# Key norms' roots taken two blocks at a time, and a pair's four loads issued at four points of the recurrence

## What is computed

```
r = (xr @ w_r)
k = (xk @ w_k)
v = (xv @ w_v)
kk = kf * k_k
kk = kk / jnp.maximum(jnp.sqrt(jnp.sum(jnp.square(kk), axis=-1, keepdims=True)), 1e-12)
k_dir = kf[None] * (1.0 + (a_rate - 1.0) * k_a)
y_f = wkv7_scan(r, decay[0], k_dir[0], v, -kk, kk * a_rate[0], reverse=False)
y_b = wkv7_scan(r, decay[1], k_dir[1], v, -kk, kk * a_rate[1], reverse=True)
# wkv7_scan, for each head of 64 channels:
#   sa = S @ a_t;  S = S * w_t + sa b_t^T + v_t k_t^T;  y_t = S @ r_t
```

## Time and profile before

| | us |
|---|---|
| median of 3 runs | 1931.05 (1930.81 to 1932.45) |
| the profiled execution, its own time | 1928.18 |
| its span in the trace | 1926.4 |
| PE busy | 1859.2 (97%) |
| DVE busy | 1055.7 (55%) |
| ACT busy | 755.4 (39%) |
| projections of k and v | about 895 to 1000 |
| recurrence | about 1000 to 1370 |

### The profile page before, as it was taken

The page is one execution under the profiler, slowest core; times in us unless marked ns, Lnnn a source line. Parts: engine busy times, 40 slices in busy tenths (PEclk is TensorE's granted clock), DMA queues, the critical chain, the costliest instruction groups (busy, mean ns, idle before and its releaser), DMA issues.

```text
span 1926.4 us, 38666 instructions
## 1 busy us (share of the span) xinstructions
PE 1859.2 (97%) x17053; PEld 1529.8 (79%) x17053; DVE 1055.7 (55%) x1405; ACT 755.4 (39%) x1006; POOL 174.2 (9%) x136
## 2 busy tenths in 40 slices
PE   6999899999999999999999999999999999999997
PEld 4898558778888888775679898899787788888886
DVE  5897665444432443447648888787664344324422
ACT  4434674334421332323844343343643353213322
POOL 1000002000000000210003211111120010000000
PEclk9999999999999999999999999999999999999999
DMA  6227223112332232443441111112352132332221
GB/s 213 84 72 233 77 99 131 66 44 91 106 110 87 88 110 90 153 137 126 153 140 50 50 50 51 50 47 69 125 197 88 33 99 87 110 103 88 94 88 44
DMA packets 165503, 189.41 MB, mean 98 GB/s; under 512 B 11801, under 2 KB 152646, under 8 KB 163674
## 3 DMA queue, kind: packets, MB, share of 16 engines
q1 hardware_dynamic: 162016, 174.44, 28.2%
q0 software_dynamic: 3088, 12.45, 1.6%
q10 hardware_dynamic: 234, 0.06, 0.0%
HBM read 161.22 MB, written 21.51 MB: 95 GB/s over the span
## 4 chain that ended last, share of the span: by engine, by line
PE 48%; DVE 5%; issue 2%; ACT 2%; DMA 0%; ACTq 0%; DVEq 0%; SPq 0%
PE ps L357 10%; PE ps L359 10%; PE ps L358 10%; PE ps L2353 7%; PE ps L2319 2%; PE ps L2366 2%; PE ps L2307 1%; PE ps L1743 1%; PE ps L2330 1%; PE ps L1313 1%; PE ps L2412 1%; PE ps L2449 1%; PE ps L1294 1%; DVE s_inverse_t L2683 1%; PE ps L2286 1%
## 5 line engine op out<-in xcount | busy, mean ns | idle before, releaser
L344 DVE TENSOR_TENSOR weights_split<-w,weights_split 128x2048 fp32r<-128x2048 f32 x116 | 265.7, 2290 | 235.3 <-ACT weights_split L326 230.5
L326 ACT ACTIVATE weights_split<-w 128x2048 fp32r<-128x2048 f32 x118 | 225.5, 1911 | 288.7 <-PE ps L359 270.2
L357 PE MATMUL ps<-x_hn_hi,weights_split 128*128 128x512 f32 x640 | 252.7, 395 | 0.0
L359 PE MATMUL ps<-x_hn_hi,weights_split 128*128 128x512 f32 x640 | 249.2, 389 | 0.0
L358 PE MATMUL ps<-x_hn_lo,weights_split 128*128 128x512 f32 x640 | 249.0, 389 | 0.0
L357 PE MATMUL ps<-f_hidden_hi,weights_split 128*128 128x512 f32 x512 | 199.3, 389 | 0.0
L359 PE MATMUL ps<-f_hidden_hi,weights_split 128*128 128x512 f32 x512 | 199.2, 389 | 0.0
L358 PE MATMUL ps<-f_hidden_lo,weights_split 128*128 128x512 f32 x512 | 199.2, 389 | 0.0
L1563 DVE SCALAR_TENSOR_TENSOR f_relu<-ps,x_squares 128x512 f32<-128x512 f32 x64 | 44.1, 691 | 191.1 <-PE ps L359 172.5
L358 PEld LDWEIGHTS ps<-x_hn_lo,weights_split 128*128 128x128 f32 x640 | 120.2, 188 | 26.2 <-issue 1.4
L357 PEld LDWEIGHTS ps<-x_hn_hi,weights_split 128*128 128x128 f32 x640 | 120.2, 188 | 26.0 <-issue 1.4
(11 more groups left out here) (365 smaller groups left out, 3513.6 us busy)
## 6 DMA issues: line engine op xcount, KB each, us to landing
w<-in_ffn_w_up_dram SPq DMA_DIRECT2D x32, 1024.0 KB, 5.4
w<-in_ffn_w_down_dram SPq DMA_DIRECT2D x32, 1024.0 KB, 4.8
w<-in_xattn_w_kv_dram SPq DMA_DIRECT2D x15, 1024.0 KB, 5.5
w<-in_ab_w_in_dram SPq DMA_DIRECT2D x10, 1024.0 KB, 5.0
w<-in_xattn_w_q_dram SPq DMA_DIRECT2D x8, 1024.0 KB, 4.9
w<-in_xattn_w_o_dram SPq DMA_DIRECT2D x8, 1024.0 KB, 4.7
w<-in_ab_w_out_dram SPq DMA_DIRECT2D x4, 1024.0 KB, 5.3
w<-in_rwkv_w_r_dram SPq DMA_DIRECT2D x4, 1024.0 KB, 6.5
```

What stands on the lines that cost most here:

```text
L326: act.activation(hi, raw, ACT.Copy).then_inc(k.w_hi_ready, 1)
L344: eng.tensor_tensor(lo, raw, hi.bitcast(F32), ALU.subtract).then_inc(k.w_lo_ready, 1)
L357: pe.matmul(out, lhs[0], rhs[0], start=start, stop=False)
L359: return pe.matmul(out, lhs[1], rhs[0], start=False, stop=stop)
```

## The change

There are two edits.

1. In the projections ACT no longer takes a root in every step t from 2 to 9. In the odd steps 3, 5, 7 and 9 it takes two, of blocks t - 3 and t - 2: Ln, Ln, one wait for both, Exp, Exp. DVE's multiplication of a key block by its root moves from step b + 3 to b + 4.
2. In the recurrence the four loads of a pair q no longer stand together at `bn` of pair q - 2. v stays there; kk is issued at `ua` of pair q - 2, r at `ub` of pair q - 2, and k at `qb` of pair q - 1, each after a wait for that copy. For q = 0 and 1 nothing changes.

```
-                if 2 <= t < 10:
+                if 3 <= t < 11 and t % 2:
 
-                    b = t - 2
-                    k.wait_freed(act, num[("n", b)])
-                    k.act.link(act, act.activation(rn[:, b % 4, :], rn[:, b % 4, :], ACT.Ln))
-                    act.activation(rn[:, b % 4, :], rn[:, b % 4, :], ACT.Exp, scale=-0.5).then_inc(s_rt, 1)
+                    b = t - 3
+                    for n in (b, b + 1):
+                        k.wait_freed(act, num[("n", n)])
+                        k.act(act.activation(rn[:, n % 4, :], rn[:, n % 4, :], ACT.Ln))
+                    k.act.wait(act)
+                    for n in (b, b + 1):
+                        act.activation(rn[:, n % 4, :], rn[:, n % 4, :], ACT.Exp, scale=-0.5).then_inc(s_rt, 1)
...
-                if 3 <= t < 11:
-                    b = t - 3
+                if 4 <= t < 12:
+                    b = t - 4
                     dve.wait_ge(s_rt, b + 1)
                     dve.tensor_tensor(kk[:, b, :], kk[:, b, :], rn[:, b % 4, :], ALU.mult).then_inc(s_kk, 1)
...
-def load_pair(k, sp, p):
+def load_pair(k, sp, p, rows=range(4)):
 
-    for a, src in enumerate((k.d_r, k.d_kk, k.d_k, k.d_v)):
+    for a in rows:
+        src = (k.d_r, k.d_kk, k.d_k, k.d_v)[a]
         sp.dma_start(k.pin[:, p % 2, a, :], src[:, p, :]).then_inc(k.s_pin[p % 2], 16)
...
                     if p + 2 < C:
                         full(sp, "VT", p)
-                        load_pair(k, sp, p + 2)
+                        load_pair(k, sp, p + 2, [3])
+                elif kind in ("ua", "ub", "qb"):
+
+                    q = p + 1 if kind == "qb" else p + 2
+                    if 2 <= q < C:
+                        taken(sp, kind.upper(), p)
+                        load_pair(k, sp, q, [{"ua": 1, "ub": 0, "qb": 2}[kind]])
```

## The result

The changed kernel takes 1949.72 us (median of 5 runs, 1944.13 to 1952.55) beside 1932.45 us for the kernel before (1930.81 to 1936.07). The ratio is 1.0083, with a 95% interval of 1.0059 to 1.0106: 0.6 to 1.1% slower, some 16 us by the ratio (the medians lie 17.3 apart). The forecast was 1939 with a range of 1930 to 1952. The span of the profiled execution went from 1926.4 to 1943.3 us, by 16.9.

The account below looks back on a forecast made before the run. PE, busy for 97% of the span, was taken to bound the kernel. The terms -5.0 + 13.7 + 3 - 2 - 2 = +7.7 us on 1931.05 gave about 1939 us, with a range of 1930 to 1952.

Parts of the forecast that it names:

- the likeliest case: Whole kernel: the forecast's own case, all five terms summing to +7.7 us, 1935 to 1946 us; chance 0.55.
- Edit 1, -5.0: Projections, at v0: fewer table loads on ACT save 3.3 us of waiting and 1.7 us of half clock, -5.0 us.
- The walk's five starts: Projections: ACT's roundings of t = 3 to 7 predicted to start at 919.8, 928.7, 933.0, 941.9 and 946.2.
- Edit 2, k's landing before VT, +13.7: Recurrence, six periods: VT waits for k's load, issued behind `qb` and landing 2.7 us later; +13.7 us.
- The clock, +3: Recurrence, behind PE's standstills before VT: the clock falls twice, each costing up to 1.7 us; +3 us, bounds 0 and 10.2.
- DVE gets ahead, -2: Recurrence: DVE gets ahead while PE stands at VT, so PE's 3.4 us of waits for it shrink; -2 us.
- The pauses inside jobs, -2: Recurrence: three PE pauses, read as instructions late behind transfer bursts, shrink as one of six transfers leaves; -2 us.
- A: Rival, recurrence: clock falls at every VT and loads land like the one behind a store; +22.3, 1953 us; chance 0.13.
- B: Rival, projections: edit 1 gives nothing because v0 waits for something other than the last split; +12.7, 1944 us; chance 0.10.
- C: Rival, recurrence: PE would have lost the standstill at VT elsewhere anyway, 9 us return; -0.3, 1931 us; chance 0.12.
- D: Rival, recurrence: all 11.6 us of empty time and one clock fall return, 13.3 us; -4.6, 1926.5 us; chance 0.10.

Follow-up runs that it names:

- edit 1 alone: The kernel before with only the paired roots and the key multiplication one step later, loads of a pair as before: ratio 0.9969 to the kernel before, 1927.95 us.
- edit 2 alone: The kernel before with only the loads of a pair issued at bn, ua, ub and qb, roots as before: ratio 1.0100 to the kernel before, 1951.57 us.
- k at `x01`: The changed kernel with the load of k issued a step later, behind x01 of pair q - 1: ratio 1.0161 to the kernel before, 1966.94 us.

## Why the prediction was right, and where it was not

The forecast's sign and mechanism held, and the result lies in its range of 1930 to 1952, but near its upper end and outside the 1935 to 1946 of the likeliest case; 1939 was 11 us too low, of which 1.4 are the median of the kernel before, 1932.45 with five runs instead of 1931.05 with three. Four of the five terms were wrong in the same direction, toward a smaller slowdown, so it is the width of the range that held the result. Point by point:

- **Edit 1, -5.0.** Measured -5.1 at the first VT (-4.8 without what was there at 800), and 0.31% or 6.0 us in the runs of edit 1 alone. The walk's five starts were within 0.3 us. That the sum agrees to 0.1 us is partly luck, since the start of the first VT scatters by 3 us between profiles. A third of it came without any wait removed, from the clock behind v0 (up to 1.7 us; v0 itself starts 3.5 us earlier).
- **Edit 2, k's landing before VT, +13.7.** Measured +14.9. SP's reaction was 0.02 to 0.04 us, and five of six landings were near the 2.7 of the load that had nothing ahead of it; the last took 3.4.
- **The clock, +3.** This is the term that was mis-sized most. The step said that the standstills lie between 1.99 and 2.65 and took two falls of 3.4 us. They were 2.49 to 2.67 long, nearly at the upper row, and the lower clock lasted 13.6 us more than before, which is up to +6.8. One of its four stretches, 3.4 us, follows a pause inside a job and not a standstill.
- **DVE gets ahead, -2.** Measured 0: twelve waits of 3.5 us in sum after, 3.4 before. They are still twelve, of at most 0.4 us each, so the head start of DVE at VT does not reach them; why not was not tried.
- **The pauses inside jobs, -2.** Measured about 0 (6.1 us after, 6.4 before). Taking k out of the burst left three loads and two stores there. The reading of the cause, which no row proved then, was right; the size for one load of four was not.

The sum of what was measured, -5.1 + 14.9 + 6.8 + 0 - 0.3 = +16.3, stands beside 16.9 between the two spans. Of the rivals, A with 1953 was the nearest in time and B's 1944 the next; of A's two conditions the clock came true in part (6.8 of its 10.2 us), the slower landings in one period of six. B fell with v0's start at 947.48; C and D fell because almost nothing of the standstill came back.

## What to carry to other kernels

When DMAs of one group are issued at different points but raise one semaphore, the first reader of any of them waits for the last of all: look which reader comes first after the last issue, and give it a semaphore of its own. In the time of a short wait of PE, count the lower clock behind it too; here it added 6.8 us to 14.9. Where PE pauses inside a job and nothing in the code holds it, look at the instruction queue's packets and at what other transfers were issued 3 to 5 us earlier. The version that came out of this, roots in pairs, v on its own semaphore at `gb` and r, kk and k at `qb`, is 0.70% faster than the kernel before (0.58 to 0.82%), and faster than the changed one by 1.5% by the two ratios.

## What the runs showed of the hardware that was not expected

- Bursts of DMAs can starve PE of instructions. Burst and pause cost 6 to 8 us in this kernel, without any data dependence between them. All 61 pauses of this kind in the thirteen profiles end 2.2 to 3.0 us after an instruction packet starts.
- Standstills of PE of nearly the same length did and did not bring the clock down. In the changed kernel it fell at 2.67, 2.63 and 2.60 us and stayed at 2.57, 2.53 and 2.49; behind 1.99 it fell there once, and in the kernel before it stayed. In the kernel with edit 2 alone the order is not even kept: it fell at standstills of 2.66 and 2.72 us and at pauses inside jobs of 2.26 and 2.59, and stayed at full speed behind 2.60, 2.61, 2.69 and 2.82. So between 2.0 and 2.8 us the length of a standstill alone does not tell whether the clock falls; behind each of six of 4.2 to 4.4 us (k at `x01`) it did.
